# Odd attention of a two-layer decoder step: scores of two heads as a pair of 64-row products, with the keys read where they lie

## The reference, cut to what matters

```python
# branch "s" (selected blocks: all 8 blocks of 64 keys can be chosen, so it is causal), queries qn
s = einsum('btgrd,bjgd->btgrj', qn, ks) * 64**-0.5 - slope * dist          # keys 0 .. t
# branch "w" (window of 256 keys), queries qn, keys kw
# branch "d" (the 128 best keys of an indexer, as a mask in the table), queries qd, keys kd
p = masked_softmax(s);  o = einsum('btgrj,bjgd->btgrd', p, v)
# per head: o_n = gate0*o_compressed + gate1*o_s + gate2*o_w ;  o_d
y = concat(o_n, o_d) @ w_out_o
```

## Time and profile before

| | us |
|---|---|
| median of 3 runs | 1476.47 |
| runs, lowest to highest | 1474.69 to 1478.83 |
| the profiled execution, its own time | 1469.87 |
| span of the profile, first to last instruction | 1468.3 |
| PE busy | 1406.6 (96%) |
| DVE busy | 794.6 (54%) |
| ACT busy | 498.8 (34%) |
| POOL busy | 404.2 (28%) |
| mean granted clock of TensorE | 0.993 |

### The profile page before, as it was taken

One profiled execution on the slowest core, in us unless ns is written; L12 is line 12 of the kernel. 1 busy time (PEld: TensorE's weight loads), 2 busy tenths in 40 slices (PEclk: granted clock), 3 DMA queues, 4 the chain that ended last, 5 costly groups with the idle time before them and its releaser, 6 DMA issues. The chain is left out here.

```text
span 1468.3 us, 27182 instructions
## 1 busy us (share of the span) xinstructions
PE 1406.6 (96%) x11095; PEld 1330.6 (91%) x11095; DVE 794.6 (54%) x1378; ACT 498.8 (34%) x992; POOL 404.2 (28%) x470
## 2 busy tenths in 40 slices
PE   6999998999999999999899899999999999999996
PEld 5999975999999999999899767788999999999996
DVE  3425868586334343346699857656485343343435
ACT  3322123354222132234432445665454033130311
POOL 3014523473010020127635460022663010010102
PEclk9999999999999999999999989999999999999998
DMA  4433170032231312304231162202133132231311
GB/s 151 133 99 115 33 230 4 3 116 76 98 115 59 116 66 108 111 12 98 91 58 40 27 211 72 59 1 58 62 111 116 59 115 100 74 116 58 115 29 59
DMA packets 87195, 123.84 MB, mean 84 GB/s; under 512 B 24438, under 2 KB 42302, under 8 KB 87040
## 3 DMA queue, kind: packets, MB, share of 16 engines
q1 hardware_dynamic: 82048, 107.00, 22.6%
q0 software_dynamic: 5024, 15.10, 3.4%
HBM read 115.62 MB, written 8.57 MB: 85 GB/s over the span
## 5 line engine op out<-in xcount | busy, mean ns | idle before, releaser
L1026 PE MATMUL ps<-xh,ring_lo 128*128 128x260 f32 (+2 forms) x2496 | 503.5, 283 | 1.4 <-ACT big L1601 1.4
L1026 PEld LDWEIGHTS ps<-xh,ring_lo 128*128 128x128 f32 (+2 forms) x2496 | 382.6, 187 | 3.3 <-ACT big L1601 2.3
L1026 PE MATMUL ps<-xh,wr 128*128 128x260 f32 x1568 | 353.7, 284 | 6.5 <-POOL ring_lo L772 2.8
L1026 PE MATMUL ps<-xl,wr 128*128 128x260 f32 x1568 | 351.3, 283 | 6.0 <-DVE xl L2056 3.6
L1026 PEld LDWEIGHTS ps<-xh,wr 128*128 128x128 f32 x1568 | 256.2, 188 | 9.3 <-issue 5.0
L1026 PEld LDWEIGHTS ps<-xl,wr 128*128 128x128 f32 x1568 | 255.3, 188 | 8.0 <-DVE xl L2056 4.9
L825 POOL TENSOR_TENSOR att<-att 128x520 f32<-128x520 f32 (+1 forms) x80 | 77.4, 968 | 548.6 <-DVE att L1982 521.3
L1958 DVE TENSOR_TENSOR ring_lo<-ring,wr 128x1024 fp32r<-128x1024 f32 (+1 forms) x144 | 192.0, 1337 | 64.4 <-ACT wr L1601 64.3
L1026 PE MATMUL ps<-hh,wr 128*128 128x260 f32 x1024 | 222.1, 283 | 0.0
L1026 PE MATMUL ps<-hh,ring_lo 128*128 128x260 f32 x1024 | 221.8, 283 | 0.0
L1026 PE MATMUL ps<-hl,wr 128*128 128x260 f32 x1024 | 221.7, 283 | 0.0
(11 more groups left out here) (351 smaller groups left out, 1775.3 us busy)
## 6 DMA issues: line engine op xcount, KB each, us to landing
ring<-in_w_up SPq DMA_DIRECT2D x16, 2048.0 KB, 8.0
ring<-in_w_down SPq DMA_DIRECT2D x16, 2048.0 KB, 7.9
ring<-in_w_in_e SPq DMA_DIRECT2D x9, 1024.0 KB, 5.3
ring<-in_w_in_e SPq DMA_DIRECT2D x2, 2048.0 KB, 8.7
ring<-in_w_out_e SPq DMA_DIRECT2D x2, 2048.0 KB, 9.1
ring<-in_w_in_o SPq DMA_DIRECT2D x16, 256.0 KB, 5.1
ring<-in_cache_kv POOLq DMA_DIRECT2D x32, 128.0 KB, 2.4
ring<-in_w_out_o SPq DMA_DIRECT2D x8, 512.0 KB, 8.3
```

What stands on the lines that cost most here:

```text
L1026: last = pe.matmul(bank(g, half)[0:width(g), 0:H2], w[:, k, :], x[:, k, cols(half)], start=first, stop=final)
```

## The change

The scores of heads (g=0, p) and (g=1, p) become a pair. Each product has a contraction of 64 rows: group 0 multiplies rows 0 to 63 of the query tile with rows 0 to 63 of the key tile in `big`, group 1 rows 64 to 127 with rows 64 to 127. A product wider than two key blocks is cut after the second one, and the pieces of the two heads are issued alternately: group 0 keys 0-1, group 1 keys 0-1, group 0 the rest, group 1 the rest. The two heads write to the two score banks as before. A pair is issued at every second step (odd t), where before one unit was issued at every step, and it waits for `q_sc >= u`: DVE must have read the scores of unit u-1 as well. The orders `turns` and `last_turns` now take two units of one query block and then two of the other. The zero-padded copies `KZ`, POOL's clearing of their area, its three pairs of copies with their waits and the semaphore `kz_ok` go away.

```diff
-        KZ = {n: att[:, 1024 * i:1024 * (i + 1)].rearrange("p (g k) -> p g k", g=2) for i, n in enumerate(("kd", "ks", "kw"))}
...
-        turns = [0, 1] * NH
-        last_turns = [0, 1, 0, 0, 1, 0, 0, 1, 0, 0, 1, 0, 1, 1, 1, 1]
+        turns = [0, 0, 1, 1] * NP
+        last_turns = [0, 0, 1, 1, 0, 0, 0, 0, 1, 1, 0, 0, 1, 1, 1, 1]
...
             pool.wait_ge(sm["xl_v"], len(XL_DVE) * 4)
-            pool.memset(kiz[:, :, :], 0.0)
-            pool.memset(att[:, 0:3072], 0.0).then_inc(sm["z_pool"], 1)
-            pool.wait_ge(sm["z_pool"], 1)
...
+            pool.memset(kiz[:, :, :], 0.0).then_inc(sm["z_pool"], 1)
...
-            padded(0, "kd")
             for name in O_NAMES[Z["qd0"]:Z["vw"] + 1]:
                 low_part(split_of[G_IN1 + Z[name]])
             low_part(split_of[G_IN1 + Z["qn0"]])
-            padded(1, "ks")
             low_part(split_of[G_IN1 + Z["qn1"]])
             low_part(split_of[G_IN1 + Z["qn2"]])
-            padded(2, "kw")
             low_part(split_of[G_IN1 + Z["qn3"]])
...
-            def unit_scores(u):
-                i, p, g, br, k0, o = units[u]
+            def pair_scores(u):
+
+                i, p, _, br, k0, o = units[u]
+                q = L[f"q{'d' if br == 'd' else 'n'}{p}"]
                 if u >= 2:
-                    pe.wait_ge(sm["q_sc"], u - 1)
-                if u == 0:
-                    pe.wait_ge(sm["kz_ok"], 2)
-                if u == first_of[4]:
-                    pe.wait_ge(sm["kz_ok"], 6)
-                mm(ps[u % 2][:, 0:P * (i + 1 - k0)], big[:, L[f"q{'d' if br == 'd' else 'n'}{p}"], P * i:P * i + P],
-                   KZ["k" + br][:, g, P * k0:P * (i + 1)]).then_inc(sm["q_mm"], 1)
+                    pe.wait_ge(sm["q_sc"], u)
+                ends = sorted({min(i + 1, k0 + 2), i + 1})
+                for c0, c1 in zip([k0] + ends, ends):
+                    for g in range(2):
+                        r = slice(HD * g, HD * g + HD)
+                        last = mm(ps[(u + g) % 2][:, P * (c0 - k0):P * (c1 - k0)], big[r, q, P * i:P * i + P],
+                                  big[r, L["k" + br], P * c0:P * c1])
+                        if c1 == i + 1:
+                            last.then_inc(sm["q_mm"], 1)
...
-            unit_scores(0)
-            unit_scores(1)
+            pair_scores(0)
...
-                if 1 < t + 1 < len(units):
-                    unit_scores(t + 1)
+                if t % 2 and t + 1 < len(units):
+                    pair_scores(t + 1)
```

More of the change, by code:

```diff
@@ L151, in build @@
             free_b sq_done sum_r mu_ok cen_p y_split x_ready xl_p hid_lo hid_sq u_ok sp_ok outs
-            c_new store_c nnew_ev ucol_ev p_raw p_ok cn_ev z_pool kiz_ok kz_ok mm_a mm_b cw_ok tm_a
+            c_new store_c nnew_ev ucol_ev p_raw p_ok cn_ev z_pool kiz_ok mm_a mm_b cw_ok tm_a
             tm_b tms_ev cmp_mm pvs_mm x_hi xl_v hid_hi stats_mm tin_a tin_b tin xe_v xe_p fg_mm rows_ok h12_mm
@@ L894, in _ @@
             pool.wait_ge(sm["xl_v"], len(XL_DVE) * 4)
-            pool.memset(kiz[:, :, :], 0.0)
-            pool.memset(att[:, 0:3072], 0.0).then_inc(sm["z_pool"], 1)
-            pool.wait_ge(sm["z_pool"], 1)
-            def tile_ready(name):
-                pool.wait_ge(sm["free_a"], G_IN1 + Z[name] + 1)
-                pool.wait_ge(sm["free_b"], G_IN1 + Z[name] + 1)
+            pool.memset(kiz[:, :, :], 0.0).then_inc(sm["z_pool"], 1)
             pool.wait_ge(sm["page_in"], 16)
```

## The result

The changed kernel takes 1498.01 us in the median of 4 runs (1491.13 to 1509.26), beside 1475.58 for the kernel before (4 runs, 1473.91 to 1478.83): a ratio of 1.016, 95% interval 1.0123 to 1.0197. Forecast were 1479 us and 1470 to 1491. The profiled execution of after is its longest, 1509.26 us, so the differences read from it are larger than those of the medians.

A forecast was written before the change was run, and what follows sets the result against it. PE, busy 96% of the span, was taken as the bound, with DVE largely setting the pace from 819 to 850 us. Terms -2.8 - 1 - 12.0 + 16.0 + 1 + 1.5 = +2.7 us gave 1479 us, range 1470 to 1491.

The forecast's parts named there:

- Term 1: Projection: without POOL's clearing and copies, PE's wait for qd0's low part goes, -2.8 us, and DVE's chain shortens, -1.
- the prediction's -1: DVE's chain of best keys gets shorter without POOL's other two pairs of copies: -1 us, bounds 0 and -2.
- Term 2: Score products after 850 us: the two heads' 64-row halves partly overlap, -12.0 us, bounds 0 and -20.5.
- the rival of full overlap: Score pairs: a pair costs what one head cost, term 2 becomes -20.5, 1471 us; chance 15%.
- Term 3: Switching PE between 128 and 64 rows for score pairs: 0.40 us each, 40 pairs, +16.0 us.
- Terms 4 and 5: First 16 units (819 to 850 us), later second pair: +1; pairs waiting until unit u-1's scores are read: +1.5.
- Theory B: Posed for the experiments, not forecast: the new order and later wait leave PE idle; no size or chance.
- theory A: Posed for the experiments, not forecast: side-by-side 64-row products, or their short streams, let the clock fall; no chance.
- the rival in which the halves don't overlap: Score pairs: group 1's records start only after group 0's, term 2 is 0, +14.7, 1491 us; chance 18%.

The follow-up runs named there:

- experiments 12 and 13: The kernel before with only POOL's clearing and kd copies moved behind the low parts PE waits for, run on two occasions: 1471.23 us and 1472.77 us.
- experiment 3: The kernel before with one extra 64-row product ahead of every second score product, 48 excursions: 1504.08 us.
- Experiments 1 and 2: The kernel before, 128-row products kept: first with the pairs' order, pairwise issue and later wait, 1484.66 us; second with the new order alone, 1478.64 us.
- experiment 9: The kernel with new order, pairwise issue and later wait on 128 rows, each score product but the first pair's streaming only half its columns: 1485.67 us.
- experiment 7: The changed kernel with every side-by-side score pair issued twice into the same banks: 1496.84 us.
- experiment 8: The changed kernel with one 128-row product of the pair's whole width ahead of each pair: 1518.18 us.
- experiment 11: The kernel before with new order, POOL's part moved, and side-by-side pairs with later wait only for 18 wide pairs from the 25th unit: 1488.48 us.
- experiment 4: The kernel before with every score product on its 64 rows, one head at a time, old order and wait: 1584.63 us.

## Why the prediction was wrong

**Term 1 was right in kind and half in size.** The wait for POOL's low part went, but the first addition came 1.9 us earlier where 3.8 were forecast, and at least 2.8 for the wait alone. The part missed is what POOL's earlier work meets. Four DVE copies (`index_keys`) that ahead of it took 1.77 us now take 5.94, and PE waits for the copy behind them. Before, then DVE and PE after:

```profile
718.43 1.77 DVE L2461 COPY att<-big 32x512 f32<-32x512 f32 x4 [2.42 <-POOL att L896]
```

```profile
716.66 5.94 DVE L2447 COPY att<-big 32x512 f32<-32x512 f32 x4
```

```profile
723.22 0.48 PE L967 MATMUL ps<-ident,big 60*128 60x60 f32 x5 [1.27 <-DVE big L2462]
```

The two copies before POOL's first low part take 0.42 us each, the two beside it 2.5. So qd0 begins at 723.62 instead of 724.68, and DVE's chain starts 1.0 us earlier, not 2.8; the other 0.9 us come behind 775 us, where two more pairs of POOL's copies are gone, which fits the prediction's -1. The kernels of experiments 12 and 13 are 4.7 and 2.6 us under before in the medians, 3.7 and 3.4 by the ratios.

**Term 2 was mis-sized.** It took a middle course, -12.0; the records start together, which is the bound, -20.5, and the rival of full overlap (given 15%). The argument against it ("the second needs the rows of the first") did not hold: the second record's load for one half goes in beside the other half's. The Trainium skill (TensorE: Matmul & The Clock Gate, Part 3, Packing small matmuls) has such starts about 4 ns apart; the trace agrees with 5 to 7 ns.

**Term 3 was right**: 0.40 us forecast, and 0.40 seen, both in the pairs of the kernel after and in experiment 3. Together with term 2 this makes -4.5 us at full clock, to which the 0.8 us gained between the 37th and the 65th unit fit: 7 pairs of three blocks and 7 of one, 28 x 0.213 = 6.0 saved and 14 x 0.40 = 5.6 paid.

**Terms 4 and 5 were too small.** Both are the later wait; together +2.5 with bounds to +9. Experiments 1 and 2 give about 6.0, of which the clock's share in experiment 1 is a part. The mechanism was named rightly: a DVE that is late stops PE at once. What was missed is which DVE work comes between: the eight small copies, 4.92 us. The kernel before has them too, in 5.50 us, and PE's longest wait on DVE's additions there is 2.2.

**The step that failed is the sum itself.** It took each product's length from rows at the clock of 0.99 and let the saved columns come off the time, as if the clock were given. It is not: after has 109 us of its attention at 1.2 GHz where before has 10. Put together from the other measurements, the change gives -1.9 (term 1) - 4.5 (terms 2 and 3) + 6.0 (the wait, with some clock in it) + 3 (the order, by a median that its interval doesn't tell from nothing) = about +3 us. That this is close to the forecast's +2.7 is luck: term 2 saved 8.5 us more than forecast, while term 1 saved 1.9 less and the wait and the order cost 6.5 more. Measured were +22.4. The rest, about 20 us, is put down to the clock by subtraction: 99 us more at half speed could cost up to 50, in a profiled execution that is itself 11 us above the median, and where DVE sets the pace it costs less. Theory B thus holds for 6 to 10 us, theory A for the rest. The prediction had no term and no rival for the clock. That the range's upper end (1491) lay near is owed to the rival in which the halves don't overlap, which is refuted; it was the right size for the wrong reason.

The sign of a fall was in the earlier trace rows: a clock of 0.88 in the one stretch where PE was not full. I read it as a sign that DVE sets the pace, and not as a price that a leaner stream would pay elsewhere.

**What stays open.** In the steady part the cause is shown from both sides: taking score columns away brings on the falls on 128 rows too (experiments 1 and 9), adding them back makes most of them go (7 and 8). Which feature of the thinner stream does it is not parted. PE's waits come with it: 5.6 of 145 us in after, 3.6 before, 3.7 in experiment 7, and after's falls at 911.96 and 976.81 come within 2 us of a wait of 0.6 us. But waits are not needed, as the last section shows, and the kernel before has its 3.6 us of them and no fall there. For the start it is only partly known. With the first 24 units issued as of old it is 14 us (experiment 11), which points to the first units' pairing and the later wait; but with the pairwise issue its length ran from 14 to 61 us over eight kernels, and the 61 came in experiment 8, whose stream is as full as that of experiment 7 with 20. Once at half clock the clock stayed there with PE busy all the time; what ends such a stretch no run here isolates. How long the falls are changes from run to run of one kernel, so the stretches quoted are each one execution.

## What to carry to other kernels

Price a saving on TensorE at both of its clock levels: in a kernel that is 96% busy there, a shorter stream between waits and switches can be answered by a lower granted clock, and here that took back about as much as the 20.5 us that the overlap saved. Read the clock beside the busy time in every stretch that the change touches, since busy time stayed at 100% where the clock was halved. And look for the by-product: the unglamorous part, moving POOL's clearing out of the way of what PE waits for, was the only one that made the kernel faster, 0.24%, and it needed none of the rest.

## What the runs showed of the hardware

- Two products on rows 0 to 63 and 64 to 127 into two banks run fully beside each other, f32 records and loads included: 5 to 7 ns between starts, and 0.63 us for two heads of two blocks where one head alone has 0.43 and the switching 0.20.
- An excursion from 128 to 64 rows and back costs 0.40 us, beside the product itself (the pairs of after, experiment 3).
- The granted clock can fall with PE recorded as busy throughout. In experiment 3 PE has no idle time from 905 us to 1050, and the clock falls at 1027.37. The windows just ahead of it and at half clock:

```profile
1017.00:1027.30 10.30, 10.30 (x73) 8.93 (x74) 6.61 (x19) 4.50 (x15) 0.00 (x0) 1.00 0.00 0
1027.40:1041.00 13.60, 13.60 (x54) 11.58 (x53) 4.85 (x14) 3.31 (x10) 0.00 (x0) 0.50 0.12 34
```

  And it stays down with PE busy, here in the kernel after:

```profile
976.00:994.00 18.00, 18.00 (x83) 15.10 (x79) 6.35 (x14) 6.93 (x18) 2.34 (x1) 0.53 0.01 2
```

  The Trainium skill (TensorE: Matmul & The Clock Gate, Part 1) says that the clock follows how busy TensorE has lately been. By the profile's busy time the trace does not agree: it is 10.30 of 10.3 us ahead of this fall, and 20.00 of 20 at half clock in experiment 4.
- Score products on 64 rows, one head at a time (96 switches), cost more clock than half of the score columns gone on 128 rows: 0.930 to 0.932 over the span in three executions of experiment 4, 0.965 to 0.975 in experiment 9.
- DVE copies of 32 rows by 512 columns took 0.42 us alone and 2.5 us each beside POOL's low parts.
